# Who adds the squares: GpSimd's additions in place of TensorE's column groups, in a decoder trunk on one core

## The reference, cut to what matters

```python
def rmsnorm(x, g):
    xf = x.astype(jnp.float32)
    y = xf * lax.rsqrt(jnp.mean(xf * xf, axis=-1, keepdims=True) + EPS)
    return (y * g.astype(jnp.float32)).astype(x.dtype)
...
        hp = hp + rmsnorm(yp, g_post_mix[i])
        fp, cvp = conv_ffn(rmsnorm(hp, g_pre_ffn[i]), ffn_w_up[i], ffn_conv_w[i], ffn_conv_b[i], ffn_w_down[i], ...)
        hp = hp + rmsnorm(fp, g_post_ffn[i])
        hp = hp + ple_term(hp, p_prompt[i], g_ple[i], ple_w_gate[i], ple_w_proj[i])
```

## Time and profile before

| | us |
|---|---|
| median of 3 runs | 1296.57 |
| lowest, highest | 1296.37, 1296.8 |
| span of the profiled execution | 1294.8 |
| TensorE busy | 1287.4 |
| VectorE busy | 891.1 |
| ScalarE busy | 594.0 |
| GpSimd busy | 75.0 |

### The profile page before, as it was taken

The page is one execution under the profiler, slowest core; times in us unless marked ns, Lnnn a source line. Parts: engine busy times, 40 slices in busy tenths (PEclk is TensorE's granted clock), DMA queues, the critical chain, the costliest instruction groups (busy, mean ns, idle before and its releaser), DMA issues.

```text
span 1294.8 us, 25277 instructions
## 1 busy us (share of the span) xinstructions
PE 1287.4 (99%) x10786; PEld 1254.7 (97%) x10786; DVE 891.1 (69%) x1602; ACT 594.0 (46%) x1060; POOL 75.0 (6%) x117
## 2 busy tenths in 40 slices
PE   9999999999999999999999999999999999999998
PEld 8999989999999999999999978999999999999998
DVE  7899776987777774223897787688777777422385
ACT  6214565544444443223855677554444444222381
POOL 1112230000100000000031020000000000000000
PEclk9999999999999999999999999999999999999999
DMA  5435521213343233222314232311322323322231
GB/s 199 155 100 194 198 99 53 103 58 106 95 105 94 87 111 114 90 90 78 138 59 148 68 97 81 113 52 50 98 94 87 98 84 110 114 90 90 79 130 67
DMA packets 35616, 131.84 MB, mean 102 GB/s; under 512 B 4516, under 2 KB 5260, under 8 KB 35184
## 3 DMA queue, kind: packets, MB, share of 16 engines
q1 hardware_dynamic: 29664, 111.33, 26.8%
q0 software_dynamic: 5408, 18.26, 4.3%
q10 hardware_dynamic: 432, 0.64, 0.2%
HBM read 121.26 MB, written 10.08 MB: 101 GB/s over the span
## 4 chain that ended last, share of the span: by engine, by line
PE 95%; DVE 3%; ACT 1%; DMA 0%; issue 0%; ACTq 0%; DVEq 0%
PE tile L1177 24%; PE tile L1181 24%; PE tile L1179 24%; PE tile L1187 5%; PE tile L1188 5%; PE tile L1189 4%; PE tile L1649 1%; PE side L1187 1%; PE side L1188 1%; PE side L1189 1%; PE sums L1226 0%; DMA raw<-in_w_kv 0%; PE sums L1700 0%; PE sums L1348 0%; PE sums L1707 0%
## 5 line engine op out<-in xcount | busy, mean ns | idle before, releaser
L756 ACT ACTIVATE wH<-raw 128x1024 fp32r<-128x1024 f32 (+1 forms) x190 | 210.9, 1113 | 377.4 <-DMA raw<-in_w_up 145.9
L1177 PE MATMUL tile<-xH,wH 128*128 128x260 f32 x1798 | 362.7, 283 | 0.1
L1181 PE MATMUL tile<-xH,wL 128*128 128x260 f32 x1798 | 362.4, 283 | 0.0
L1179 PE MATMUL tile<-xL,wH 128*128 128x260 f32 x1798 | 361.8, 283 | 0.0
L1832 DVE TENSOR_TENSOR wL<-raw,wH 128x1024 fp32r<-128x1024 f32 (+1 forms) x190 | 245.7, 1294 | 154.5 <-ACT wH L756 150.4
L1177 PEld LDWEIGHTS tile<-xH,wH 128*128 128x128 f32 x1798 | 277.1, 188 | 3.5 <-issue 3.0
L1181 PEld LDWEIGHTS tile<-xH,wL 128*128 128x128 f32 x1798 | 277.2, 188 | 0.0
L1179 PEld LDWEIGHTS tile<-xL,wH 128*128 128x128 f32 x1798 | 276.4, 188 | 0.0
L1880 DVE SCALAR_TENSOR_TENSOR u<-tile,rstd 128x520 f32<-128x520 f32 x96 | 67.2, 700 | 119.5 <-PE tile L1181 119.4
L1177 PE MATMUL tile<-hidH,wH 128*128 128x260 f32 x616 | 124.3, 283 | 0.0
L1181 PE MATMUL tile<-hidH,wL 128*128 128x260 f32 x616 | 123.8, 282 | 0.0
(11 more groups left out here) (446 smaller groups left out, 1913.9 us busy)
## 6 DMA issues: line engine op xcount, KB each, us to landing
raw<-in_w_up SPq DMA_DIRECT2D x88, 512.0 KB, 3.6
raw<-in_w_down SPq DMA_DIRECT2D x32, 704.0 KB, 4.1
raw<-in_w_ple SPq DMA_DIRECT2D x16, 512.0 KB, 5.6
raw<-in_w_qo SPq DMA_DIRECT2D x12, 512.0 KB, 3.6
raw<-in_w_qkv SPq DMA_DIRECT2D x12, 512.0 KB, 3.5
raw<-in_w_kv SPq DMA_DIRECT2D x10, 512.0 KB, 3.7
cring<-in_c_in POOLq DMA_DIRECT2D x8, 512.0 KB, 4.8
out_c_s<-cring POOLq DMA_DIRECT2D x8, 512.0 KB, 3.2
```

Of the source, the lines that this page charges most:

```text
L756: nc.scalar.activation(wH[j][:, 0:n], raw[j][:, 0:n], ACT.Copy).then_inc(s_high, 1)
L1177: nc.tensor.matmul(out[:, q, 0:HT], wh, x[0][:, k, tokens(q)], start=first, stop=False)
L1179: nc.tensor.matmul(out[:, q, 0:HT], wh, x[1][:, k, tokens(q)], start=False, stop=False)
L1181: mm = nc.tensor.matmul(out[:, q, 0:HT], wl, x[0][:, k, tokens(q)], start=False, stop=last)
```

## The change

`GROUPED` becomes `FOLDED`. For the six sums GpSimd adds the eight tiles of squares into the first, seven additions of 128x260 f32, each waiting for the next square and for the addition before it. TensorE then does one sum over one tile as in up's first half, at the place where `square_sum` stood; `square_group` and ScalarE's `group_sums` go, and `pre_root` divides by D throughout. In GpSimd's queue the fold of up stands behind the memset of `u` and ahead of the cache copies, the two of ple behind the load of `pin`.

```diff
@@ -105,7 +105,7 @@
 ROOT = {("kv", 0): 1, ("mout", 0): 2, ("mout", 1): 3, ("down0", 0): 4, ("down0", 1): 5, ("qkv", 0): 6,
         ("sout", 0): 7, ("sout", 1): 8, ("down1", 0): 9, ("down1", 1): 10}
 PREROOT = {(s, q): 2 * i + q + 1 for i, s in enumerate(("up0", "ple0", "up1", "ple1")) for q in range(2)}
-GROUPED = {sq: n + 1 for n, sq in enumerate(sq for sq in PREROOT if sq[0][:2] != "up" or sq[1])}
+FOLDED = {sq: n + 1 for n, sq in enumerate(sq for sq in PREROOT if sq[0][:2] != "up" or sq[1])}
 POST = {"up0": "mout", "ple0": "down0", "up1": "sout", "ple1": "down1"}
 G_PRE_MIX, G_POST_MIX, G_PRE_FFN, G_POST_FFN, G_PLE = range(5)
 
@@ -330,7 +330,7 @@
                                                           sem("gate_weights_ready"), sem("gate_parts_read"),
                                                           sem("gate_rows"), sem("gate_rows_read"))
         s_part, s_sqadd = sem("gate_parts_done"), sem("squares_added")
-        s_psum, s_psumr = sem("pre_squares_by_group"), sem("pre_squares_by_group_read")
+        s_pooled, s_folds = sem("pre_squares_added_by_pool"), sem("pool_fold_steps")
         s_fold = sem("pre_squares_added")
         s_raw0 = [sem(f"first_weights_in{c}") for c in range(2)]
         s_high0, s_low0 = sem("first_weights_high"), sem("first_weights_low")
@@ -700,6 +700,20 @@
             pool.wait_ge(s_out, 16 * stored)
             pool.wait_ge(s_cps, 16)
 
+            folds = Chain(pool, s_folds)
+
+            def fold_squares(stage, q):
+
+                total = square(stage, q, 0)
+                pool.wait_ge(s_sq, SQ0[stage] + KT * q + 2)
+                for k in range(1, KT):
+                    if k > 1:
+                        pool.wait_ge(s_sq, SQ0[stage] + KT * q + k + 1)
+                    step = nc.gpsimd.tensor_tensor(total, total, square(stage, q, k), ALU.add)
+                    if k < KT - 1:
+                        folds.link(step)
+                step.then_inc(s_pooled, 1)
+
             for layer in range(NL):
                 up, down, ple = f"up{layer}", f"down{layer}", f"ple{layer}"
 
@@ -711,6 +725,7 @@
 
                 pool.wait_ge(s_afin if layer == 0 else s_rope, NH + 1 if layer == 0 else 2 + KT)
                 nc.gpsimd.memset(u[:, :, 0:2], 0.0).then_inc(s_pad, 1)
+                fold_squares(up, 1)
                 if layer == 0:
                     for i, (r0, r1) in enumerate(COPIES):
                         pool.wait_ge(s_mm, CHUNK0["up0"] + 4 * i + 4)
@@ -723,6 +738,8 @@
                 stored += 1
 
                 pool.dma_start(pin[:], g.p[layer]).then_inc(s_p, 16)
+                for q in range(2):
+                    fold_squares(ple, q)
                 if layer == 0:
                     pool.wait_ge(s_mm, CHUNK0["ple0"] + 1 + NEXTRA)
                     nc.gpsimd.memset(qpad[:], 0.0).then_inc(s_qz, 1)
@@ -770,12 +787,7 @@
 
                 act.wait_ge(s_squ, KT + PREROOT[stage, q])
                 nc.scalar.activation(rstd[:, tokens(q)], sums[:, q, 0:HT], ACT.Sqrt, bias=eps[:, 0:1],
-                                     scale=1.0 / (32 * D if (stage, q) in GROUPED else D)).then_inc(s_rootp, 1)
-
-            def group_sums(stage, q):
-
-                act.wait_ge(s_psum, GROUPED[stage, q])
-                nc.scalar.activation(square(stage, q, 0), sums[:, q, 0:HT], ACT.Copy).then_inc(s_psumr, 1)
+                                     scale=1.0 / D).then_inc(s_rootp, 1)
 
             def inputs(stage, k, q, layer, norm):
 
@@ -951,7 +963,6 @@
                     inputs(up, k, 1, layer, G_PRE_FFN)
                     if k == 2:
                         high(up, 3)
-                group_sums(up, 1)
                 pre_root(up, 1)
                 high(up, 4)
                 high(up, 5)
@@ -1026,7 +1037,6 @@
                 p_copy(5)
                 high(ple, 1)
                 ple_input(0, 1)
-                group_sums(ple, 0)
                 p_copy(6)
                 high(ple, 2)
                 ple_input(1, 1)
@@ -1037,7 +1047,6 @@
                 for k in range(4, KT):
                     ple_input(k, 1)
                 high(ple, 3)
-                group_sums(ple, 1)
                 high(ple, 4)
                 pre_root(ple, 1)
                 for c in range(5, KT):
@@ -1217,23 +1226,12 @@
                 elif r + k0 >= 2:
                     pe.wait_ge(s_read, r + k0 - 1)
 
-            def square_group(stage, q, part):
-
-                pe.wait_ge(s_sq, SQ0[stage] + KT * q + 4 * part + 4)
-                if part == 0:
-                    pe.wait_ge(s_root, ROOT[POST[stage], q])
-                for j in range(4):
-                    mm = nc.tensor.matmul(sums[32 * j:32 * j + 32, q, 0:HT], ones[:, 0:32], square(stage, q, 4 * part + j),
-                                          start=(part == 0), stop=(part == 1), skip_group_check=True)
-                if part:
-                    mm.then_inc(s_psum, 1)
-
             def square_sum(stage, q):
 
-                if (stage, q) in GROUPED:
-                    pe.wait_ge(s_psumr, GROUPED[stage, q])
+                pe.wait_ge(s_root, ROOT[POST[stage], q])
+                if (stage, q) in FOLDED:
+                    pe.wait_ge(s_pooled, FOLDED[stage, q])
                 else:
-                    pe.wait_ge(s_root, ROOT[POST[stage], q])
                     pe.wait_ge(s_fold, int(stage[2]) + 1)
                 nc.tensor.matmul(sums[:, q, 0:HT], ones, square(stage, q, 0), start=True, stop=True).then_inc(s_squ, 1)
 
@@ -1529,8 +1527,6 @@
                 for k in range(4):
                     for c in range(SPLIT):
                         second_half(up, c, k, k + 1)
-                square_group(up, 1, 0)
-                square_group(up, 1, 1)
                 for c in range(2):
                     second_half(up, c, 4, 5)
                 square_sum(up, 1)
@@ -1587,9 +1583,6 @@
                         mm.then_inc(s_mm if jj == 3 and q == 1 else s_pw, 1)
                     if j == 0:
                         y_sum(down, 1)
-                    if j == 5:
-                        square_group(ple, 0, 0)
-                        square_group(ple, 0, 1)
 
                 yd = YREAD0[down]
                 square_sum(ple, 0)
@@ -1599,8 +1592,6 @@
                 for k in range(3):
                     for c in range(SPLIT):
                         second_half(ple, c, k, k + 1)
-                square_group(ple, 1, 0)
-                square_group(ple, 1, 1)
                 for c in range(SPLIT):
                     second_half(ple, c, 3, 4)
                 square_sum(ple, 1)
```

## The result

The changed kernel takes 1301.43 us (median of 4 runs, 1301.29 to 1301.54), the kernel before 1296.53 beside it: 1.0037 times as long (95% interval 1.0025 to 1.0049), 4.9 us slower. The forecast was 10.2 us slower; the sign and the range held, the size was twice what came. The profiled execution's span is 1299.6 us (before 1294.8), its time 1301.42.

The account below looks back on a forecast made before the run. TensorE, busy 99% of the span, was taken to bound the kernel, but VectorE to decide in up. Up's +7.2 us and the embedding's +3.0 gave +10.2: 1296.57 + 10.2 = 1306.8 us, range 1299.5 to 1311.5.

Parts of the forecast that it names:

- What bounds, and that TensorE's 1.21 us are worth nothing in up: In up VectorE decides when chunk 5 starts, so the 1.21 us a group leaving TensorE there win nothing.
- One add, 0.75 us: One GpSimd addition of 260 columns takes 0.75 us, bounds 0.6 to 1.0; seven make one fold.
- The exclusion: VectorE operations with two SBUF inputs and GpSimd instructions reading SBUF exclude each other for whole operations and take turns.
- Rival 1: No exclusion for these short adds: up wins nothing, the embedding 1.8 us a layer; 1293.0 us, chance 0.13.
- Rival 2: Small holds of 0.35 us: up loses 4.2 us, the embedding comes out near zero; 1300.8 us, chance 0.12.
- Rival 3: GpSimd kept out while VectorE runs without a gap, so folds end late: +11.6 us, 1308.2 us, chance 0.15.
- The hold, 0.60: Each add taking its turn in VectorE's gapless residual pushes VectorE back 0.60 us, bounds 0.35 and 0.9.
- Six pushes a fold: In up, adds 1 to 6 meet VectorE's residual steps, the seventh a reciprocal: 3.6 us a layer, +7.2 in all.
- The embedding, +1.5 a layer: In the embedding, holds make chunk 3 start later: +1.5 us a layer, +3.0 in all, bounds -1.8 and +4 a layer.
- the gaps: Three idle gaps of VectorE in the embedding's first half take 1.7 of 3.6 us of pushes; 1.9 remain.
- the room of 1.35: In the embedding, 1.35 us between the end of VectorE's read of chunk 0 and the start of chunk 3.
- No contention, -1.8 a layer in the embedding: Without contention the embedding wins 0.6 us in its first half and 1.21 in its second: -1.8 us a layer.

Follow-up runs that it names:

- experiment 4: Changed kernel, but in up GpSimd's adds became memsets of up to 780 columns and TensorE summed the first tile of squares alone: 1295.96 us.
- experiment 3: Changed kernel, but in up TensorE summed the last tile of squares alone and waited for GpSimd's adds only at chunk 3: 1302.83 us.
- experiment 10: Changed kernel, but GpSimd folded only up's second half, starting when the last square was there; the embedding was grouped as before the change: 1308.88 us.
- experiments 7 and 8: Changed kernel, TensorE not waiting for GpSimd's adds in up until chunk 3; all adds of half width (1295.16 us), or one-input copies of full width (1294.74 us).
- experiment 2: Changed kernel, but GpSimd folded only up's second half and the embedding kept TensorE's column groups: 1302.03 us.

## Why the prediction was right in direction and wrong in size

- **What bounds, and that TensorE's 1.21 us are worth nothing in up: right.** With the holds gone (experiment 4) they reappear as TensorE's wait for VectorE at chunks 3 and 5. In the changed kernel itself the wait is at the sum (2.2 us a layer), and chunk 3 didn't wait: the forecast had waits at both.
- **One add, 0.75 us: right** (0.74).
- **The exclusion: right.** It is shown by the 0.97 us steps, by the memsets that push nothing, and by the pushes' following the length of GpSimd's instruction. Rival 1 falls. Rival 2 (a hold of 0.35, the embedding near zero, 1300.8 us) came nearer than the forecast: the hold lies between the two, and the embedding is as rival 2 had it. Rival 3's waiting at the sum is there (2.2 us a layer), but it costs nothing (experiment 3), and VectorE's steps, not the adds, are the ones held for long. Rival 3's mechanism has to be forced, as in experiment 10, to be seen.
- **The hold, 0.60: too large, first failed term.** I took "0.1 at its end, less some 0.05 of start" from one pair of 512 columns. Three sizes show 0.25 for a 0.48 us step: the start was right, but 0.20 of the step, not 0.1, passes while it is held. That is 0.50 an add.
- **Six pushes a fold: five and a half.** The larger part of the sixth falls into the wait for ScalarE in front of the last low part (0.18 us idle before the change). 5 pushes of 0.49 to 0.55 plus 0.2 are 2.75 a layer, where the forecast had 3.6. Over two layers this is 1.7 of the 5.3 us of error.
- **The embedding, +1.5 a layer: wrong, the larger failed term; it was -0.34.** The first half's residual ends 0.53 late where 1.9 was reckoned. Five pushes were 2.2 to 2.3 together, one of them on a weight's low part (1.66 for 1.22), and the gaps took 1.66, as forecast: 3.6 was the wrong number, not 1.7. In the second half the pushes come to 2.66, not 3.6. I had used VectorE's free moment at 642.1 plus 5.5 of delay, 3.3 late; it was 0.88. The rest of that working held: 0.88 less the room of 1.35 is -0.47, and chunk 3 came 0.4 early. The forecast was pushes of 7.2 us less a slack of 5.3 (1.7 + 2.22 + 1.35); with pushes of 4.9 the difference is -0.4, so an error of a third in the pushes turned the sign. This term is 3.7 of the 5.3.
- **No contention, -1.8 a layer in the embedding: right in size**, by experiments 7 and 8 (-1.65).
- **Not seen ahead:** TensorE's clock, below; it made chunk 3 later but not chunk 5, and so cost the changed kernel nothing that the traces show.

What stays open: that a held step does all its columns behind GpSimd's end is read from three widths, and no run was made to test it. The rule of 0.25 us is measured for GpSimd instructions of 0.41 to 0.74 us beside VectorE steps of 0.48 us, and not beyond.

## What to carry over

Work taken from the busiest engine wins only in the stages where no other engine's chain runs level with it, so look at each stage's last wait before counting it. GpSimd's help is not free beside a VectorE that runs two-input operations without a gap: here each GpSimd instruction that read SBUF (0.41 to 0.74 us) cost VectorE its own length less 0.25 us, and where the sum was forecast as pushes less slack, the slack made a small error in the hold a large one in the result. The place for such adds was the engine that was already waiting there: VectorE, in front of the embedding's last reciprocal (1294.19 us).

## What the runs showed of the hardware beyond what was expected

- A GpSimd copy with one input pushes VectorE's two-input steps as well (0.14 us), by the same rule as an add; a memset of 0.75 us doesn't. The Trainium skill (SBUF — State Buffer, SBUF: two separate sides) says that the first of the two has the shared pair for the whole instruction and the other fully blocks. The ends of the held rows agree (0.28, 0.56 and 1.09 us behind GpSimd's end for 260, 512 and 1024 columns); the price is still 0.25 us less than the instruction, for the reason given under experiments 7 and 8.
- TensorE's granted clock fell to the lower of its two levels (1.2 of 2.4 GHz) behind waits of about 2 us, and in experiment 10 within one of 5.2. The changed kernel, first layer, windows:

```profile
246.00:248.00 2.00, 0.19 (x1) 0.22 (x2) 2.00 (x3) 0.65 (x2) 1.26 (x2) 0.89 0.00 0
248.00:250.00 2.00, 2.00 (x8) 1.81 (x9) 1.97 (x4) 0.94 (x2) 0.00 (x0) 0.50 0.00 0
250.00:252.00 2.00, 2.00 (x15) 2.00 (x15) 2.00 (x2) 1.43 (x2) 0.00 (x0) 0.76 0.00 0
```

TensorE was idle for 2.2 us, then its matmuls started 0.22 us apart in place of 0.12 for some 3 us. That made TensorE late for chunk 3: it came at 253.39, where VectorE's read had freed the bank at 252.91. It did no harm, since chunk 5 waited for VectorE anyway, at 265.16, 2.74 behind the earlier trace rows. In experiment 2 the same wait of 2.22 us, in the first layer, left the clock at 1.00, and chunk 3 waited 0.89 for VectorE:

```profile
246.00:248.00 2.00, 0.06 (x1) 0.09 (x1) 2.00 (x3) 0.79 (x2) 1.39 (x2) 1.00 0.00 0
248.00:250.00 2.00, 2.00 (x15) 1.94 (x16) 1.97 (x4) 1.34 (x3) 0.00 (x0) 1.00 0.00 0
```

In its second layer the clock fell all the same. Where the fall comes behind chunk 3, nothing covers it. Experiment 3, TensorE and windows:

```profile
252.70 0.48 PE L1186 MATMUL tile<-xH,wH 128*128 128x260 f32 x2 [1.94 <-issue]
...
254.23 0.64 PE L1190 MATMUL tile<-xH,wL 128*128 128x260 f32 x2
```

```profile
254.00:256.00 2.00, 2.00 (x11) 2.00 (x11) 1.97 (x5) 0.76 (x1) 0.00 (x0) 0.50 0.26 98
```

Its one run with a mean clock of 1.000 took 1301.42 us, the four with 0.997 to 0.999 took 1302.6 to 1303.2: about 1.4 us. Five runs tie the 1.4 us to the clock, no run of its own does. A wait that is harmless in itself can so cost time by what follows it.
